# Matmuls without a reader on TensorE while it waits: ends of sublayers, norm sums of the mixers, end of the gated-delta sublayers

## What is computed

```
def _rmsnorm(x, g):
    xf = x.astype(jnp.float32)
    y = xf * lax.rsqrt(jnp.mean(xf * xf, axis=-1, keepdims=True) + EPS)
    return (y * g.astype(jnp.float32)).astype(x.dtype)
...
def _swiglu(x, w_up, w_down):
    g, u = jnp.split(x @ w_up, 2, axis=-1)
    return (jax.nn.silu(g) * u) @ w_down
...
        x = x + 0.5 * _rmsnorm(_swiglu(_rmsnorm(x, ng[0]), w_ffn_up[layer, 0], w_ffn_down[layer, 0]), ng[1])
...
        x = x + _rmsnorm(h, ng[3])
        x = x + 0.5 * _rmsnorm(_swiglu(_rmsnorm(x, ng[4]), w_ffn_up[layer, 1], w_ffn_down[layer, 1]), ng[5])
```

## Time and profile before

| | us |
|---|---|
| median of 3 runs | 2816.47 |
| lowest, highest | 2815.74, 2819.28 |
| the profiled execution | 2812.93 |
| its span, first to last instruction | 2811.2 |

### The profile page before, as it was taken

The page is one execution under the profiler, slowest core; times in us unless marked ns, Lnnn a source line. Parts: engine busy times, 40 slices in busy tenths (PEclk is TensorE's granted clock), DMA queues, the critical chain, the costliest instruction groups (busy, mean ns, idle before and its releaser), DMA issues.

```text
span 2811.2 us, 51786 instructions
## 1 busy us (share of the span) xinstructions
PE 2674.3 (95%) x22016; PEld 2509.7 (89%) x22016; DVE 1547.3 (55%) x1978; ACT 1154.2 (41%) x1515; POOL 273.4 (10%) x294
## 2 busy tenths in 40 slices
PE   7998999899999899999999989999999989988998
PEld 7997887899999886699999978799999978877998
DVE  5546835655555445465465543465555558446554
ACT  4334444444433344343344333343343335435432
POOL 1000004100100225110010000010010000042000
PEclk9999999999999999999999999999999999998999
DMA  5544532454544535444455453455455444134543
GB/s 192 164 146 132 150 85 66 153 164 147 166 163 142 187 114 164 136 143 161 147 171 165 138 168 108 128 166 164 147 168 164 139 144 150 57 101 143 165 142 100
DMA packets 415626, 404.23 MB, mean 144 GB/s; under 512 B 14786, under 2 KB 411950, under 8 KB 415086
## 3 DMA queue, kind: packets, MB, share of 16 engines
q1 hardware_dynamic: 411348, 397.42, 44.9%
q0 software_dynamic: 4096, 4.20, 0.5%
HBM read 385.19 MB, written 16.39 MB: 143 GB/s over the span
## 4 chain that ended last, share of the span: by engine, by line
PE 88%; DVE 7%; ACT 2%; POOL 2%; issue 1%; DMA 0%; SPq 0%; DVEq 0%; POOLq 0%; ACTq 0%
PE psum L351 22%; PE psum L352 22%; PE psum L353 22%; POOL fbuf L406 1%; DVE x L537 1%; DVE y L535 1%; PE psum L2641 1%; PE psum L389 1%; PE psum L1115 1%; PE psum L1098 1%; PE psum L984 1%; DVE xn_lo L470 1%; PE psum L2040 1%; DVE w_lo L333 1%; PE psum L985 1%
## 5 line engine op out<-in xcount | busy, mean ns | idle before, releaser
L333 DVE TENSOR_TENSOR w_lo<-raw,w_hi 128x2048 fp32r<-128x2048 f32 (+3 forms) x366 | 753.4, 2058 | 555.5 <-ACT w_hi L326 555.4
L351 PE MATMUL psum<-xn_hi,w_hi 128*128 128x288 f32 x3296 | 987.2, 300 | 20.4 <-DVE xn_lo L1690 7.5
L352 PE MATMUL psum<-xn_lo,w_hi 128*128 128x288 f32 x3296 | 978.6, 297 | 0.0
L353 PE MATMUL psum<-xn_hi,w_lo 128*128 128x288 f32 x3296 | 975.2, 296 | 0.0
L326 ACT ACTIVATE w_hi<-raw 128x2048 fp32r<-128x2048 f32 (+3 forms) x366 | 623.9, 1705 | 785.2 <-PE psum L353 720.9
L351 PEld LDWEIGHTS psum<-xn_hi,w_hi 128*128 128x128 f32 x3296 | 623.9, 189 | 31.7 <-issue 16.4
L353 PEld LDWEIGHTS psum<-xn_hi,w_lo 128*128 128x128 f32 x3296 | 626.8, 190 | 0.0
L352 PEld LDWEIGHTS psum<-xn_lo,w_hi 128*128 128x128 f32 x3296 | 625.4, 190 | 0.4
L352 PE MATMUL psum<-h_lo,w_hi 128*128 128x288 f32 x1408 | 415.5, 295 | 0.0
L353 PE MATMUL psum<-h_hi,w_lo 128*128 128x288 f32 x1408 | 415.0, 295 | 0.0
L351 PE MATMUL psum<-h_hi,w_hi 128*128 128x288 f32 x1408 | 413.3, 294 | 0.0
(11 more groups left out here) (561 smaller groups left out, 3126.1 us busy)
## 6 DMA issues: line engine op xcount, KB each, us to landing
raw<-w_ffn_up SPq DMA_DIRECT2D x176, 1024.0 KB, 5.1
raw<-w_ffn_down SPq DMA_DIRECT2D x64, 768.0 KB, 4.4
raw<-w_ffn_down SPq DMA_DIRECT2D x64, 640.0 KB, 4.0
raw<-gdn_w_in SPq DMA_DIRECT2D x32, 1024.0 KB, 5.7
raw<-mlstm_w_in SPq DMA_DIRECT2D x12, 1024.0 KB, 5.4
raw<-gdn_w_out SPq DMA_DIRECT2D x8, 1024.0 KB, 6.8
raw<-cache_mla_latent SPq DMA_DIRECT2D x64, 128.0 KB, 2.2
a_split<-cache_mla_latent SPq DMA_DIRECT2D x64, 128.0 KB, 2.3
```

Source lines behind the costliest of these rows:

```text
L333: dve.tensor_tensor(wview(w_lo[slot(u, i)], u), wview(raw[u % NRAW], u), wview(w_hi[slot(u, i)], u).bitcast(F32), ALU.subtract).then_inc(l ...
L351: pe.matmul(out, wh[:, k, c], hi(k), start=st, stop=False)
L352: pe.matmul(out, wh[:, k, c], lo(k), start=False, stop=False)
L353: last = pe.matmul(out, wl[:, k, c], hi(k), start=False, stop=sp_)
```

## The change

`pe_filled(pe, u, bank, count)` waits until ScalarE has rounded unit `u`, and then runs `count` matmuls with the unit's first 128 columns as weights and 288 other columns of it as the moving side, into a bank that nobody reads before it is written anew. They signal nothing. They are called

- at the end of every sublayer but the last, behind `pe_leave_sums`: 19 matmuls into bank 2, once VectorE has copied the first half of the products to `y`;
- behind a mixer's norm sums (`pe_sum_squares`): 14, into bank 2;
- in a gated-delta sublayer ahead of the last two sets of output transposes: 10, into bank 1, once ScalarE has copied all state updates out of it; and behind the transposes: 16.

All of it is on TensorE's queue; no other engine's program changes.

```diff
--- before.py
+++ after.py
@@ -406,6 +406,13 @@
                 pool.tensor_tensor(sq_part, sq_part, sq[:, 2 * i:2 * i + 2, :], ALU.add).then_inc(sum_step, 1)
             pool.wait_ge(sum_step, done + len(chunks) + 1)
             pool.tensor_tensor(sq_total, sq_part[:, 0, :], sq_part[:, 1, :], ALU.add).then_inc(sq_sum, 1)
+
+        def pe_filled(pe, u, bank, count):
+
+            pe.wait_ge(hi_ready, u + 1)
+            buf = w_hi[slot(u)]
+            for _ in range(count):
+                pe.matmul(psum[:, bank, 0:T], buf[:, 0:P], buf[:, 256:256 + T], start=True, stop=True)
 
         def pe_enter_sums(pe, n):
 
@@ -938,7 +945,11 @@
             for c in range(4):
                 chain(pe, c)
             for k in range(6):
+                if k == 4:
+                    once(pe, "g_ssu_copied", 8)
+                    pe_filled(pe, u0 + 17, 1, 10)
                 outputs_turned(pe, k)
+            pe_filled(pe, u0 + 17, 1, 16)
             once(pe, "g_s_new", 8)
             once(pe, "g_s_odd", 8)
             once(pe, "g_f", 6)
@@ -3027,7 +3038,11 @@
                 if sub[0] != "ffn":
                     for i in range(H):
                         pe_sum_squares(pe, 2 * n, i)
+                    pe_filled(pe, ubase[n], 2, 14)
                 PE[sub[0]](pe, n)
+                if n + 1 < NSUB:
+                    pe.wait_ge(y_copied, H * n + 2)
+                    pe_filled(pe, ubase[n + 1], 2, 19)
             pe.wait_ge(x_ready, entered(NSUB + 1))
             for t, (cols, _, _) in enumerate(token_tiles):
                 m = cols.stop - cols.start
```

## The result

The kernel before took 2815.8 us (median of 20 runs, 2812.2 to 2819.8), the changed one 2827.7 us (median of 20, 2817.1 to 2836.9). The ratio is 1.0043 with a 95% interval of 1.0034 to 1.0051: **slower by 0.43%**, 12 us, where 2818 and no visible change were forecast. Note the spread: 8 us before, 20 us after. The profiled execution is one of the quicker ones, with a span of 2819.3 us.

What follows compares the result with a forecast made beforehand. TensorE, busy 95% of the span, was taken to bound the kernel. The terms, +8.4 at FFN entries, -4.0 at mixer entries and -2.7 at gated-delta ends, summed to +1.7 us: 2818 us, range 2808.5 to 2824.

Steps and rivals of the forecast that it cites:

- The aim and the fillers' own cost: Sublayer ends: low clock follows TensorE's idling there; fillers at 0.13 us fit inside it and delay no real matmul.
- Term 1: Entries of the seven FFN sublayers: nothing gained, as GpSimd's sum starts 15.80 us in whatever TensorE's clock.
- Term 2: FFN entries, wait for GpSimd's sum: idling grows from 1.35 to 2.9 us, low clock follows in 8 of 10; +8.4 us.
- Terms 3 and 4: Four mixer entries, -4.0 us, and ends of gated-delta sublayers, -2.7 us: gains from fewer slow matmuls.
- or if L413 moves: FFN entries: prediction is wrong if TensorE's matmul for GpSimd's sum no longer starts 15.8 us behind the first matmul.
- The third rival: FFN entries: clock falls behind GpSimd's sum in every one, often for two stretches, 12.6 us; 2826 us, chance 0.13.

Runs made afterwards that it cites:

- e3: The change, with VectorE's second weight split at FFN entries held until GpSimd's sum of squares is done: 2820.4 us against 2818.0 for the kernel before.
- e8: The change with only the fillers ahead of FFN sublayers, plus VectorE's split waiting for GpSimd's sum: 2823.8 us against 2816.3 for the kernel before.
- e5: The change, with VectorE's split waiting for GpSimd's sum and 19 more fillers in TensorE's wait for it: 2808.6 us against 2816.3 for the kernel before.
- e4: The change, with 19 more fillers per FFN entry in TensorE's wait for GpSimd's sum: 2832.5 us against 2818.0 for the kernel before.
- e9: The change itself, run once more for a second profile: 2837.4 us against 2816.5 for the kernel before.
- e1: The change without its 19 fillers ahead of FFN sublayers, all others kept: 2815.2 us against 2818.0 for the kernel before.
- e10: The kernel before, with VectorE's split waiting for GpSimd's sum and TensorE's sum matmul moved behind 24 matmuls of the next pair: 2813.2 us against 2816.5.
- e2: The change with only its 19 fillers ahead of FFN sublayers, all others taken out: 2841.5 us against 2818.0 for the kernel before.

## Why the prediction was wrong

- **The aim and the fillers' own cost: right.** Clock 1.00 over the end of every sublayer, 0.13 us a filler, the first real matmul where it was (0.93 us of idling left). Where they stand they delay nothing: the first matmul of the first mixer starts 9.29 us behind its first norm sum, against 9.32 before.
- **Term 1, nothing gained at FFN entries: right in that.** Where GpSimd wins the toss the sum stands 15.79 us in, with the 96 matmuls slow or fast.
- **Term 2, the clock behind the sum: right, and a little low.** 2.88 us of idling were foreseen as 2.9. Of the 20 such waits in the profiles of the change, e3 and e8, 18 were followed by a low clock, where I had taken 8 in 10. The bare price by e5 against e3 is 10.1 us, against +8.4. The trace of before has two waits nearer to 2.9 us than my 2.37 that I passed over, 2.61 us at 492.2 and 2.41 at 2538.3. Each is followed within 2 us by another wait of over 3 us, so neither decides it. In e4, 2.51 us were followed by a low clock in six entries of seven. The Trainium skill ("TensorE: Matmul & The Clock Gate", "Why this matters for your kernels") asks for no idle gap of over about 3 us between bursts of matmuls. Keeping under that was not enough here: the 20 gaps, of 2.86 to 2.89 us, were all shorter.
- **Terms 3 and 4, forecast at -6.7 us: of the right sign, the size not settled (-2.8 to -7.7).** All norm sums take 5.62 us as foreseen. The mixers of the first profile are 5.3 us shorter and those of e9's 6.7, but they vary from one execution to the next. Over all twelve profiles the four mixers together take 1016.3 to 1021.2 us in the five kernels without fillers for them (mean 1019.9) and 1013.4 to 1021.3 in the seven with them (mean 1016.3), 3.6 us less. In the medians e1 wins 2.8 us (0.8 to 5.6), and e5, whose FFN sublayers are as long as before, 7.7 (4.8 to 11.5). What the sum took too lightly is the idling that the fillers leave. I had called 1.8 us at a mixer's entry safe, as 2.35 us had once done no harm. In the seven profiles with these fillers a low clock begins within 2.3 us behind it in 16 of 28 entries, as in the second mixer of the change, where 0.54 us more of idling follow and which is 1.1 us longer than before:

```profile
980.72 0.37 PE L351 MATMUL psum<-xn_hi,w_hi 128*128 128x288 f32 x1 [1.83 <-DVE xn_lo L510]
```

```profile
981.80:988.40 6.60, 6.12 (x24) 0.50 0.10 33
```

  At the ends of the gated-delta sublayers the fillers leave 1.16 and 0.87 us in the change's profile and the output projections start at clock 1.00; in e1's they leave 2.05 and 2.06 us, and both projections have a low stretch again. The single row on which "did no harm" rested was a lucky one: the same wait in the third mixer, 2.35 us for a weight split, left the clock up in the kernel before and in e8, and was followed by a low clock in the other ten profiles, with fillers (the change) and without (e10). So that fall is not owed to the fillers:

```profile
1693.81 0.37 PE L351 MATMUL psum<-xn_hi,w_hi 128*128 128x288 f32 x1 [2.35 <-DVE w_lo L333]
```

```profile
1695.10:1698.40 3.30, 3.30 (x16) 0.50 0.97 318
```

```profile
1687.57 0.37 PE L352 MATMUL psum<-xn_hi,w_hi 128*128 128x288 f32 x1 [2.34 <-DVE w_lo L333]
```

```profile
1688.60:1691.90 3.30, 3.30 (x16) 0.50 0.97 301
```

- **The step that failed is the sentence in term 1 that GpSimd's chain "hangs on VectorE and ScalarE, not on TensorE's clock".** True of its inputs, and I took it to be all. I had not followed what else becomes early when the 96 matmuls end 1.5 us sooner: they release the weight buffer, ScalarE rounds the next unit, VectorE splits it, and that split now starts together with GpSimd's last addition. In the trace that I had they were 0.74 us apart (the addition's end at 15.75, the split's start at 16.49), less than the 1.5 us that were to be won. The missing term is 3.0 us for each lost toss, 0 to 21 us in a run. With the collision taken out (e3) the change stands at +2.4 us, near the forecast of +1.7; with it, at +12, and in e9 at +21. It makes the spread too: the two profiled executions, with one and with seven lost, have spans of 2819.3 and 2835.7 us.
- **The sign "or if L413 moves"** was the right alarm: in the lost tosses the sum stands 17.95 us in.
- The third rival named 2826 us and double low stretches, near the 2827.7 measured. It put 12.6 us on the clock. The double stretches are there, but nearly all behind a lost toss; without one there are none in e3, at 2820.4 us, and two of seven in e8. The number came out near by another cause, which is luck.

That GpSimd and VectorE block each other is stated by the Trainium skill, "SBUF — State Buffer", "SBUF: two separate sides": they share a pair of ports to SBUF, the core's on-chip memory, that one of them holds for a whole instruction, while the other waits; a VectorE operation with two inputs in SBUF takes part, against a GpSimd operation that reads SBUF. The trace agrees: 0.79 us became 2.93 behind a split of 2.29, and the split became 2.93 behind an addition of 0.79.

Left open: what sets the margin of a few ns between the two starts. The same program lost one of seven in one execution and seven of seven in another; nothing here separates the chip, the run and the instructions around it.

## What to carry to other kernels

Keeping a clock up where nobody waits for the slow work only moves the idle time to the next wait; ask where the engine will arrive early, how long it will then stand, and what stands behind that wait. Follow every semaphore that the sped-up work signals, buffers set free included, and look for two instructions of VectorE and GpSimd whose starts were apart by less than the time won. When a small change widens the spread of the runs, one profile is a sample: look for an instruction whose length differs between places that should be alike.

## What was not expected of the hardware

- A collision of VectorE and GpSimd on a margin of 0.01 us, whose loser pays nearly the other's whole length: GpSimd's 0.79 us addition takes 2.15 us more behind a split of 2.29 us.
- The clock's answer to the same idle time isn't fixed: behind 2.35 us at the same place it held in two profiles and fell in ten, behind 2.87 us it fell in five of seven entries of one execution (e8). A fall behind 2.9 us costs 1.5 us, in some cases 2.7 (e8's 222.5 against 219.8 us).
- Idling of 5.03 us left a low clock of 6.8 us and not 3.4, in all seven entries of e9 and in six of seven of e2.
